# The low part of a table tile on GpSimd: one tensor_tensor of 1,024 columns, or two of 512

## What is computed

```python
s = jnp.einsum('thpd,phnd->thpn', q, sub_keys)          # two scores of 128 keys for each head
top, pos = lax.top_k(cand, PEER_TOPK)                   # 16 of the best pairs of keys
gate = jax.nn.softmax(top, axis=-1)
a = jnp.einsum('thkd,td->thk', u_tab[eidx], xb)
act = jax.nn.gelu(a) * gate
return jnp.einsum('thk,thkd->td', act, v_tab[eidx])
```

## Time and profile before

| | us |
|---|---|
| median of 3 runs | 1717.17 |
| lowest, highest | 1716.99, 1718.45 |
| the profiled execution | 1716.78 |
| its span | 1715.0 |
| TensorE busy | 1666.8 |
| VectorE busy | 1182.1 |
| GpSimd busy | 1132.8 |
| ScalarE busy | 665.1 |

### The profile page before, as it was taken

The page is one execution under the profiler, slowest core; times in us unless marked ns, Lnnn a source line. Parts: engine busy times, 40 slices in busy tenths (PEclk is TensorE's granted clock), DMA queues, the critical chain, the costliest instruction groups (busy, mean ns, idle before and its releaser), DMA issues.

```text
span 1715.0 us, 27259 instructions
## 1 busy us (share of the span) xinstructions
PE 1666.8 (97%) x10559; PEld 1598.4 (93%) x10559; DVE 1182.1 (69%) x2276; ACT 665.1 (39%) x1055; POOL 1132.8 (66%) x677
## 2 busy tenths in 40 slices
PE   8999999899999999989999999999999999999996
PEld 3899878697999999989999999999999999999996
DVE  4340244645779689899888888446887877878745
ACT  2554222333334333333344334334444444444432
POOL 1767322132335889976766676778999798999952
PEclk9999999999999999999999999999999999999998
DMA  8645213044204889979999999979999999999951
GB/s 277 217 150 160 74 65 105 17 143 148 89 36 144 303 272 323 329 241 331 360 341 353 350 359 344 339 304 343 398 409 401 368 392 410 401 408 398 397 196 65
DMA packets 192706, 461.27 MB, mean 269 GB/s; under 512 B 21185, under 2 KB 99009, under 8 KB 192449
## 3 DMA queue, kind: packets, MB, share of 16 engines
q1 hardware_dynamic: 79872, 242.31, 40.0%
q0 software_dynamic: 46080, 167.79, 26.1%
q10 hardware_dynamic: 66624, 49.42, 8.7%
HBM read 407.64 MB, written 51.83 MB: 268 GB/s over the span
## 4 chain that ended last, share of the span: by engine, by line
PE 83%; DVE 9%; DMA 3%; POOL 3%; issue 2%; ACT 1%; SPq 0%; DVEq 0%; ACTq 0%; POOLq 0%
PE ps L929 51%; PE ps L699 18%; PE ps L940 5%; DMA tab<-in_tab 3%; PE ps L719 2%; POOL tLo L655 1%; PE ps L728 1%; DVE ug L1580 1%; PE ps L902 1%; POOL ug L665 1%; DVE ps L1590 1%; DMA raw<-in_w 1%; PE ps L834 1%; DVE eqb L1692 0%; PE ps L856 0%
## 5 line engine op out<-in xcount | busy, mean ns | idle before, releaser
L655 POOL TENSOR_TENSOR tLo<-tab,tHi 128x1024 fp32r<-128x1024 f32 x256 | 624.0, 2438 | 150.9 <-ACT tHi L1179 148.1
L1179 ACT CAST tHi<-tab 128x1024 fp32r<-128x1024 f32 x256 | 267.8, 1046 | 290.4 <-PE ps L929 210.0
L929 PE MATMUL ps<-hHi,tLo 128*128 128x384 f32 x1024 | 347.3, 339 | 4.1 <-POOL tLo L655 3.3
L929 PE MATMUL ps<-actHi,tLo 128*128 128x384 f32 x1024 | 342.8, 335 | 2.1 <-POOL tLo L655 1.4
L929 PE MATMUL ps<-hHi,tHi 128*128 128x384 f32 x1024 | 342.8, 335 | 0.0
L929 PE MATMUL ps<-hLo,tHi 128*128 128x384 f32 x1024 | 342.7, 335 | 0.0
L929 PE MATMUL ps<-actLo,tHi 128*128 128x384 f32 x1024 | 342.1, 334 | 0.0
L929 PE MATMUL ps<-actHi,tHi 128*128 128x384 f32 x1024 | 342.1, 334 | 0.0
L643 POOL TENSOR_TENSOR wLo<-raw,wHi 128x1024 fp32r<-128x1024 f32 x53 | 128.2, 2419 | 290.2 <-ACT wHi L1011 290.2
L1580 DVE SCALAR_TENSOR_TENSOR ug<-ug,ps 128x1024 f32<-128x1024 f32 x160 | 191.2, 1218 | 55.1 <-DMA ug<-in_urows,eidx 50.2
L1590 DVE SCALAR_TENSOR_TENSOR ps<-ug,act_s,ps 128x1024 f32<-128x1024 f32 x158 | 202.7, 1283 | 5.4 <-DVE ps L1590 0.5
(11 more groups left out here) (355 smaller groups left out, 2479.3 us busy)
## 6 DMA issues: line engine op xcount, KB each, us to landing
tab<-in_tab SPq DMA_DIRECT2D x256, 512.0 KB, 6.7
raw<-in_w SPq DMA_DIRECT2D x101, 512.0 KB, 4.2
gate_scratch<-stage ACTq DMA_DIRECT2D x48, 512.0 KB, 7.0
gt<-gate_scratch SPq DMA_DIRECT2D x32, 768.0 KB, 6.9
gelu_scratch<-ga ACTq DMA_DIRECT2D x112, 192.0 KB, 5.7
gin<-gelu_scratch SPq DMA_DIRECT2D x112, 192.0 KB, 9.2
ug<-in_urows,eidx POOLq DMA_INDIRECT x160, 7.0
ug<-in_vrows,eidx POOLq DMA_INDIRECT x160, 7.4
```

The costliest lines, as they stand in the source:

```text
L655: pool.tensor_tensor(tLo[:, n % SPL], tab[:, n % TABS], tHi[:, n % SPL].bitcast(F32), ALU.subtract).then_inc(s_tlo, 1)
L929: last = mm(ps[:, bank, 0:TD], w, x[:, k, 0:TD], start=first, stop=end)
L1179: nc.scalar.copy(tHi[:, n % SPL], tab[:, n % TABS]).then_inc(s_thi, 1)
```

## The change

GpSimd makes the low part of a table tile in two instructions, blocks 0 to 3 (512 columns) and then blocks 4 to 7, instead of one over all 1,024 columns. The semaphore is counted up after the second. Nothing else is changed; the low parts of the weights (L643, L649) stay in one instruction.

```diff
             def lo_part(n):
 
                 pool.wait_ge(s_thi, n + 1)
-                pool.tensor_tensor(tLo[:, n % SPL], tab[:, n % TABS], tHi[:, n % SPL].bitcast(F32), ALU.subtract).then_inc(s_tlo, 1)
+                for k in (0, KT // 2):
+                    half = slice(k, k + KT // 2)
+                    last = pool.tensor_tensor(tLo[:, n % SPL, half], tab[:, n % TABS, half], tHi[:, n % SPL, half].bitcast(F32), ALU.subtract)
+                last.then_inc(s_tlo, 1)
```

## The result

The change makes the kernel slower: median 1723.82 us (1721.62 to 1724.96, 6 runs) against 1717.08 (1715.06 to 1718.45, 6 runs), ratio 1.0037 with a 95% interval of 1.0027 to 1.0047. That is +6.7 us. The profiled execution took 1723.57 us.

The account below looks back on a forecast made before the run. TensorE (97% busy) bounds most, with GpSimd nearly the bound in the V half and already the bound at the U half's end. Terms 1.2 + 1.4 + 1.3 + 8.0 = 11.9 us on the 1717.2 median gave 1729.1; range 1716 to 1740.

Parts of the forecast that it names:

- the threshold: V half: GpSimd has 0.58 us to spare in seven steps, 0.083 us a step; added work below that is free.
- (a): Start, to 750 us: one d, 0.2; VectorE's shortened wait, -1.2; two VectorE operations slipping in on GpSimd, +2.2; together +1.2 us.
- the first and third rivals: First: price under GpSimd's spare time, some +1.5 us, chance 0.20. Third: each input costs its own, +22 us, chance 0.20.
- the second: Rival: the finer lock lets VectorE's contended operations in between halves, some 5 us faster, 1712; chance 0.06.
- d: GpSimd: the price of one more instruction beside its columns, taken as 0.18 us.
- (e): V half, the 100 steps from product 141 to the last gather (product 241): 0.097 us a step, 9.7, reduced to 8.0 us.
- (d): V half up to product 141: nothing left of tLo's lead there, the nine tLos before it add 1.6, counted as 1.3 us.
- The fold of the sample rows: V half, within (e): TensorE's extra 1.72 us on the sample rows lets GpSimd catch up once.
- (c): End of the U half, products 115 to 122: GpSimd is the bound, eight tLos at 0.18, 1.4 us.
- (b): From 750 to 1090 us: no cost, hidden under the gate products' longer steps of some 5.9 us.

Follow-up runs that it names:

- mid: Kernel before, with two halves only for tiles 51 to 112, where gate products lie between table products: 1718.47 us, ratio 1.0003.
- v_only: Kernel before, with two halves only for the tiles of the V half (128 and more): 1720.19 us, ratio 1.0019.
- quarters: Kernel before, with four instructions of 256 columns for every tile: 1758.33 us, ratio 1.0235.
- the pair of spreads: Gathers spread more evenly over the steps than in the kernel before, with one instruction a tile (1715.90 us) or two halves (1716.79 us).
- retr: Kernel before, with two halves only for tiles under 51, while VectorE picks the top 16: 1719.88 us, ratio 1.0013.
- early8: Kernel before, with two halves only for the first nine tiles (8 and less): 1716.03 us, ratio 0.9989.
- u_end: Kernel before, with two halves only for tiles 113 to 127, where each step has two gathers: 1718.66 us, ratio 1.0012.
- late_retr: Kernel before, with two halves only for tiles 9 to 50: 1721.62 us, ratio 1.0027.
- spread_early8: Kernel before, with gathers spread more evenly and two halves for the first nine tiles only: 1712.67 us, ratio 0.9980.
- the three spreads: Kernel before with more even gathers: one instruction a tile (1715.90 us), halves everywhere (1716.79 us), or halves for the first nine tiles only (1712.67 us).
- uneven: Kernel before, with every tile cut into two instructions of 896 and 128 columns: 1720.98 us, ratio 1.0024.

## Why the prediction was right, and where its terms were off

1729.1 us was forecast, in a range of 1716 to 1740; 1723.8 came, slower as forecast, with 57% of the size (+6.7 of +11.9). The range was wide enough for anything from no change to +23 us, so that it held says little; what bears the forecast out is the threshold, shown by mid, v_only, quarters and the pair of spreads. In stage (a) there was luck: both of its parts were about half of what came, and they have opposite signs.

- **The price of one more instruction** was forecast as 0.18 us, measured 0.135: pairs of 2.54 to 2.56 us against 2.41, cut evenly or 7 to 1, and 0.40 for three cuts. It is close to what affine_select's row gave, 0.13; the half of a second input's worth that I put on top is not in the runs. The 0.27 us that I had estimated from the 4,497 ns of the Trainium skill (GPSIMD Engine Reference, section 3.1) is twice what the runs show, and the first and third rivals, with d under 0.09 and at 0.27, fall with it; the second, which needed d under 0.07, falls in its size.
- **(e), the V half, was the mis-sized term**: 8.0 us forecast. Above the threshold of 0.083 a step only d - 0.083 counts, so 0.045 too much in d is nearly twice the result: with 0.135 the same formula gives (0.945 - 0.58) / 7 = 0.052 a step, 5.2 us, less 1.7, 3.5. Products 192 to 240 measured 2.18 / 48 = 0.045 a step, and v_only +3.3 us for the whole V half, (d) and (e) together, where 9.3 had been forecast. In the change's own trace products 122 to 240 are only 1.6 us longer: its tLo first comes just in time (0.15 us ahead) at product 155, not at 141, so fewer than the 100 steps of the forecast pay, and at product 172 it gains 1.2 us over before, as the last section shows.
- **The fold of the sample rows** "lets GpSimd catch up once", worth 1.7 us in the forecast. It does for three products (tLo 171 is 5.1 us ahead before), and then loses all of it: two gathers wait 3.2 us each for VectorE, and tLo 172 comes 1.4 us late (rows in the last section). That is also one of the three waits of the earlier trace rows, where the forecast saw the end of the U half; the three are at products 9, 48 and 172.
- **(c)**: 1.4 us forecast, 1.06 to 1.09 measured, eight tiles, right but for the price. GpSimd was not yet the bound at product 115, though: tLo was 4.22 us ahead there, and that lead was just used up, 0.62 us a step, at product 122.
- **(b)**: nothing forecast, nothing measured (mid), though the mean step is 5.6 us (346.15 / 62), not 5.9.
- **(a)**: +1.2 us forecast, +2.2 by retr's ratio (+1.7 by the trace of the change). The parts were right in kind and both too small: -1.0 forecast up to product 9, -1.95 measured; +2.2 after it, +3.7 measured. Of these 3.7, 1.6 are GpSimd's, by product 29: a slip-in costs it the whole of a VectorE operation, and the 4,096-column ones take 2.28 us, not the 1.1 that I took from a 2,048-column one. The other 2.1 are a term that the forecast did not have: it let VectorE only gain from halves, and the same `eqa` of the earlier trace rows took 5.97 us instead of 2.21. Nor did halves halve the longest single wait: 4.9 us behind four halves.
- **The rival that the finer lock makes it faster** was half right: it does for nine tiles (early8, 2 us), and its other side, the wait for `best`, did not shrink with halves (5.9 us against 5.4).
- I expected TensorE's waits on tLo to grow to some 13 us or be spread thinly. The second: 4.6 us in five waits against 4.7 in three. A reader who had looked at the waits alone would have found nothing.

The parts by themselves, v_only, u_end and retr, add up to 1.0044 and the change has 1.0037, inside the intervals.

## What to carry to other kernels

Ask of an engine off the critical path not its busy share but its room in each step of the steady state: here GpSimd was 66% busy in all, but 28.54 us of work in a cycle of 29.12. A fixed cost under that room is free, and above it every step pays the excess, which makes the result steep: three cuts cost six times what one did. Two engines that share a port can get in where the other's instruction ends, though here not at every end. So cutting one engine's instructions can help where the other engine is late (the nine early tiles, and product 172), and hurts where the cut engine is late itself.

Before a stretch's loss is put down to the edit, look at its granted clock: 1.6 of late_retr's 5.1 us were TensorE at 1.2 GHz.

## What the runs showed that I had not expected

- Product 0 of the table stage starts in one of two places, whatever the kernel: at 521.57 to 521.90 us in before, v_only, early8, late_retr and spread_early8, at 523.48 to 524.40 in the other eight. The list of waits tells them apart long before the changed line, in TensorE's waits for the low part of h (before the change, and after it):

```profile
PE ps L699 <- DVE hLo L1314: 2.6, 2, 1.5
```

```profile
PE ps L702 <- DVE hLo L1317: 4.1, 2, 3.0
```

  The same 2.5 to 2.6 and 4.1 come in the other profiles with the early and the late start. That is 2 us of scatter between executions, a third of the effect studied, and reason enough not to subtract two profiled spans: before to after they differ by 6.8 us, 1.75 of it from before product 0. What decides between the two is open; it was not tried.
- Products 122 to 192 scatter between 293.6 and 296.5 us among kernels with one instruction per tile there, but are 292.98 to 292.99 in all three kernels with the gathers spread. Most of it is one wait, at product 172, behind the fold of the sample rows. GpSimd's and TensorE's timelines in the kernel before:

```profile
1342.45 0.93 POOL L665 DMA_INDIRECT ug<-in_vrows,eidx  x1 [3.20 <-DVE ps L1590]
1343.40 2.38 POOL L655 TENSOR_TENSOR tLo<-tab,tHi 128x1024 fp32r<-128x1024 f32 x1
```

```profile
1345.92 0.41 PE L929 MATMUL ps<-actHi,tLo 128*128 128x384 f32 x1 [1.40 <-POOL tLo L655]
```

  The gathers wait for VectorE, and VectorE had met a tLo just before, in its addition of the fold to `xT` (before, and after the change):

```profile
1332.57 2.81 DVE L1801 TENSOR_TENSOR xT<-xT,ysm 128x256 f32<-128x256 f32 x1
```

```profile
1337.47 1.49 DVE L1804 TENSOR_TENSOR xT<-xT,ysm 128x256 f32<-128x256 f32 x1
```

  Where this addition took 2.81 to 3.05 us (before, u_end, early8, late_retr, mid), TensorE waited 1.4 to 1.6 us at product 172; where it took 0.43 (retr and the three spreads), not at all; and with halves or uneven cuts (after, v_only, uneven) it took 1.1 to 1.5, and TensorE waited 0.25 or less. So in the V half the shorter hold gives 1.2 us back.
- A tensor_tensor's duration on GpSimd in these runs is close to a straight line: 0.50 us (mean) for 128 columns, 1.30 (median) for 512, 2.16 (mean) for 896, 2.41 (median) for 1,024, so about 0.19 us and 2.2 ns a column, of which some 0.05 us overlaps with the next instruction.
